# Delta-rule inverse of a hybrid trunk layer: 32x32 blocks on five levels instead of one

## Chip, cores and metric

The kernel runs on one core of a Trainium2 chip. The time is the device time of one execution in microseconds (us), the median of three runs. A second, profiled execution gives the trace; its span is the time from its first instruction to its last.

## What is computed

The reference is one step of a network of two shared-weight layers over 512 latent and 128 context tokens (640 rows, in five tiles of 128). Each layer has four mixers: A, a chunked gated delta rule in two directions; B, long convolutions; C and D, attention. The change lies in mixer A, which has four heads. Per head, direction and chunk of 64 tokens it solves a unit triangular system:

```
lower = jnp.where(strict, jnp.einsum('bhnid,bhnjd->bhnij', kb, k) * decay, 0.0)
sol = lax.linalg.triangular_solve(lower + jnp.eye(CHUNK, dtype=jnp.float32), rhs,
                                  left_side=True, lower=True, unit_diagonal=True)
```

## The kernel before, in words

Everything is laid out by hand: each engine has its own program, written in the order in which it runs, and semaphores join them. All products with the large weights are sums of three products of split operands (`h_hi*w_hi + h_lo*w_hi + h_hi*w_lo`); the trace calls them proj<-h_hi,w_hi and so on.

Instead of solving, mixer A inverts the triangular matrices by doubling, `A_levels(h)`. Level `lv` makes the inverses of diagonal blocks of 2^(lv+1) rows out of those of 2^lv rows. A tile of 128 tokens is worked in two halves of 64 rows (`HALVES`) in both directions (`d`), so one level has 2 directions, 5 tiles and 2 halves. A level has two blocks of small fp32 matmuls on TensorE (PE). `A_level_q` makes the product of the matrix `dec` with the present inverse `Y`: 20 matmuls of 64x64. ScalarE (ACT) copies it, negated, into `Q`. `A_level_d` makes the two products of `Q` with `X`, 40 matmuls of 64x64. VectorE (DVE) then takes the new entries into `X` and `Y` with `copy_predicated` under the masks of the level (`update`, lines 2311 and 2312). Level 0 has only half of the second block (20 matmuls by the identity `ident_64`). Levels 5 and 6, which join blocks of 32 and 64 rows, have code of their own.

Up to level 4 the inverse is block diagonal in blocks of at most 32 rows, so products of 32x32 diagonal blocks (`QUARTERS`, four per tile instead of two halves) hold all that is needed; the rest of the PSUM tile `mix` lies outside the masks. The kernel before does so on level 2 (`FOURS = 2`) of heads 0 to 2, not on the others. Head 3 takes 64x64 on all these levels.

Between the blocks stand pieces of the projection of the next head, the fills: `eighths` of six 128x320 matmuls each. After the first block of a level there is one, after the second one there are two (three after level 4), after level 0 two. They cover the answers of ACT and DVE. Every fp32 matmul of the small blocks is two weight loads (PEld LDWEIGHTS) and two MATMUL instructions in the trace, so 20 matmuls of 64x64 are 40 records of each kind; a matmul of a fill is one of each. The two layers run the same program text twice in a row, unrolled, and mixer A's head loop is unrolled too.

Of the kernel before, what the change touches and what calls it, by code (L numbers as in the profile page):

```python
# [20 lines left out]
TILES, KT, HEADS, W = 5, 8, 4, 128  # L21
# [23 lines left out]
def program(nc, I, O):  # L45
# [3 lines left out]
    with ctx:  # L49
        def sb(name, shape, dt=f32):  # L50
            return ctx.enter_context(nc.sbuf_tensor(name, [shape[0], int(np.prod(shape[1:]))], dt))

        def view(t, *dims, at=0):

            n = int(np.prod(dims))
            names = "abcd"[:len(dims)]
            return t[:, at:at + n].rearrange(
                "p (" + " ".join(names) + ") -> p " + " ".join(names),
                **{x: d for x, d in zip(names[:-1], dims[:-1])}) if len(dims) > 1 else t[:, at:at + n]
# [19 lines left out]
        ident_64 = sb("ident_64", [128, 64])  # L79
# [171 lines left out]
        X, Y = a.take(2, TILES, 64), a.take(2, TILES, 64)  # L251
# [10 lines left out]
        Q, Q_mid, Q_last = view(area, 2, TILES, 64, at=a_q), view(area, TILES, 32, at=a_q), view(area, TILES, 64, at=a_q + HALF)  # L262
        SIDES = (slice(0, 64), slice(64, 128))
        HALVES = tuple((c, slice(0, 64)) for c in SIDES)
        QUARTERS = tuple((slice(32 * i, 32 * i + 32), slice(32 * (i % 2), 32 * (i % 2) + 32)) for i in range(4))
        FOURS = 2
        A_GATES = {0: (0, 3), 14: (3, 4), 18: (4, 5), 22: (5, 6)}
        A_pairs = tuple((d, QUARTERS[2 * i + d][0], QUARTERS[2 * i + 1 - d][0], QUARTERS[d][1], QUARTERS[1 - d][1])
                        for d in range(2) for i in range(2))
# [446 lines left out]
        def _(pe):  # L716
# [4 lines left out]
            def mm(out, l, r, start=True, stop=True):  # L721
                return T.matmul(out, l, r, start=start, stop=stop)  # L722
# [34 lines left out]
            for layer in range(DEPTH):  # L757
# [198 lines left out]
                def A_level_q(h, lv):  # L956

                    e = h * A_STEPS + 2 * lv
                    for d in range(2):
                        pe.wait_ge(A_x.sem, A_x.at(layer, e + (d - 1)))  # L960
                        for t in range(TILES):
                            for c, w in QUARTERS if lv == FOURS and h < HEADS - 1 else HALVES:
                                at = 1024 * d + 64 * t + w.start
                                last = mm(M[c, at:at + w.stop - w.start], dec[c, d, t, c], Y[c, d, t, w])
                        last.then_inc(A_q.sem, A_q.step)

                def A_level_d(h, lv):
                    e = h * A_STEPS + 2 * lv
                    for d in range(2):
                        pe.wait_ge(A_qn.sem, A_qn.at(layer, e + (d + 1)))  # L970
                        if lv == 0:
                            pe.wait_ge(A_q0.sem, A_q0.at(layer, h + 1))
                        blocks = QUARTERS if lv == FOURS and h < HEADS - 1 else HALVES
                        for t in range(TILES if lv else 0):
                            for c, w in blocks:
                                at = 1024 * d + 64 * t + w.start
                                mm(M[c, at:at + w.stop - w.start], Q[c, d, t, w], X[c, d, t, w])
                        for t in range(TILES):
                            for c, w in blocks:
                                at = 1024 * d + 512 + 64 * t + w.start  # L980
                                l, r = (X[c, d, t, w], Q[c, d, t, w]) if lv else (Q[c, d, t, w], ident_64[c, :])
                                last = mm(M[c, at:at + w.stop - w.start], l, r)
                        last.then_inc(A_d.sem, A_d.step)

# [39 lines left out]
                def A_levels(h):  # L1024
# [11 lines left out]
                    fill(0, 2)  # L1036
                    pe.wait_ge(A_su.sem, A_su.at(layer, 5 * h))
                    A_level_d(h, 0)
                    fill(2, 4)
                    for lv, (first, mid, end) in enumerate(((4, 5, 7), (7, 8, 10), (10, 11, 13), (13, 14, 17), (17, 18, 20), (20, 22, 24)), 1):  # L1040
                        if lv < LEVELS - 2:
                            A_level_q(h, lv)
                        elif lv == LEVELS - 2:
                            A_mid_q(h)
                        else:
                            A_last_q(h)
                        fill(first, mid)
                        if lv < LEVELS - 2:
                            A_level_d(h, lv)
                        elif lv == LEVELS - 2:  # L1050
                            A_mid_d(h)
                        else:
                            A_last_d(h)
                        if lv == 1 and h:
                            pe.wait_ge(proj_taken.sem, proj_taken.at(layer, min(4 * h + 5, 15)))
                            if h == HEADS - 1:
                                pe.wait_ge(proj_taken.sem, proj_taken.at(layer, 16))
                            A_out(h - 1, psum_a[int(h == HEADS - 1)])
                        fill(mid, end)
# [1923 lines left out]
```

## Time and profile before

| what | value |
|---|---|
| median of 3 runs | 2581.85 us |
| lowest, highest | 2580.23, 2582.1 us |
| span of the profiled execution | 2586.7 us (no other time of it is on record) |
| PE busy, share of the span | 2487.4 us, 96% |
| weight loads (PEld) busy | 2355.7 us, 91% |
| DVE, ACT, POOL busy | 1332.7, 977.9, 341.7 us |
| small matmuls of 64x64, records (without level 0) | 3440, 118.8 us |
| small matmuls of 32x32, records | 2240, 27.2 us |
| fetches on queue q8, kind "instruction" | 172, 2.82 MB |

PE, the matmuls, and PEld, the weight loads, are one instruction stream and overlap. "Idle before" is the time in which the engine did nothing ahead of an instruction; behind the arrow stands what ended it. "issue" there means that nothing in the profile, neither a semaphore nor data, was waited for. Matmuls are pipelined, so the time that a block takes is read from its start to the start of what follows it, not from its length.

### The profile page before, as it was taken

The numbers are of one execution on the slowest core, as the hardware profiler recorded it, in microseconds if no ns is written. First come the engines' busy times: TensorE is split into PE (matmuls) and PEld (weight loads), VectorE is DVE, ScalarE is ACT, GpSimd is POOL, SyncE is SP. The second block draws the span as 40 slices with busy tenths as digits, with TensorE's granted clock in tenths as the row PEclk, the third lists the DMA queues.
The fourth block names the chain that finished last, engine by engine and source line by source line (L and its number), as shares of the span: only waits on it lengthen the run. The fifth ranks groups of instructions, "written<-read, shape, count | busy, mean of one in ns | idle before, by whom it ended". The sixth has DMA issues, their size and how long they took to land. (4 is left out here: it accounts for less than half of the span.)

```text
span 2586.7 us, 56706 instructions
## 1 busy us (share of the span) xinstructions
PE 2487.4 (96%) x23368; PEld 2355.7 (91%) x23368; DVE 1332.7 (52%) x2335; ACT 977.9 (38%) x1830; POOL 341.7 (13%) x406
## 2 busy tenths in 40 slices
PE   6999989999999999999989999999999999999998
PEld 4889889999999999879988888899999999988898
DVE  4565653577434434653555566527773344356544
ACT  3545432333234424442354454233332353254422
POOL 1332211000011101110013332100000010011000
PEclk9999999999999999999999999999999999999999
DMA  7111104111234333213221100231113332222132
GB/s 262 38 39 33 36 20 145 58 35 48 103 106 98 85 107 96 64 54 141 86 82 37 39 31 31 66 120 37 50 50 92 86 89 84 84 65 71 42 108 82
DMA packets 55687, 193.89 MB, mean 75 GB/s; under 512 B 9032, under 2 KB 9198, under 8 KB 55328
## 3 DMA queue, kind: packets, MB, share of 16 engines
q1 hardware_dynamic: 40304, 147.34, 16.9%
q0 software_dynamic: 15152, 43.24, 6.3%
q8 instruction: 172, 2.82, 0.4%
q14 instruction: 59, 0.48, 0.1%
HBM read 177.97 MB, written 8.39 MB: 72 GB/s over the span
## 5 line engine op out<-in xcount | busy, mean ns | idle before, releaser
L722 PE MATMUL proj<-h_hi,w_hi 128*128 128x320 f32 x3072 | 749.6, 324 | 8.7 <-DVE h_lo L2104 5.2
L722 PE MATMUL proj<-h_lo,w_hi 128*128 128x320 f32 x3072 | 703.9, 310 | 0.0
L722 PE MATMUL proj<-h_hi,w_lo 128*128 128x320 f32 x3072 | 699.5, 310 | 0.0
L2104 DVE TENSOR_TENSOR w_lo<-raw,w_hi 128x1024 fp32r<-128x1024 f32 x232 | 289.8, 1249 | 527.6 <-ACT w_hi L1562 527.4
L722 PEld LDWEIGHTS proj<-h_hi,w_hi 128*128 128x128 f32 x3072 | 503.6, 189 | 32.0 <-issue 11.4
L722 PEld LDWEIGHTS proj<-h_lo,w_hi 128*128 128x128 f32 x3072 | 516.3, 189 | 0.0
L722 PEld LDWEIGHTS proj<-h_hi,w_lo 128*128 128x128 f32 x3072 | 514.5, 188 | 0.0
L722 PE MATMUL mix<-area 64*64 64x64 f32 (+7 forms) x8176 | 474.2, 238 | 29.4 <-DVE area L2312 12.1
L722 PEld LDWEIGHTS mix<-area 64*64 64x64 f32 (+4 forms) x8176 | 402.3, 142 | 89.1 <-issue 46.3
L1562 ACT ACTIVATE w_hi<-raw 128x1024 fp32r<-128x1024 f32 x232 | 245.6, 1059 | 587.1 <-PE proj L722 397.3
L1562 ACT ACTIVATE area<-mix 128x384 f32<-128x384 f32 (+8 forms) x422 | 186.8, 466 | 570.1 <-PE mix L722 415.3
L2104 DVE TENSOR_TENSOR area<-area 128x512 f32<-128x512 f32 (+6 forms) x234 | 159.4, 712 | 29.1 <-ACT merged L2031 14.3
L476 POOL TENSOR_TENSOR stat<-stat,neg_half 128x5 f32<-128x5 f32 (+2 forms) x40 | 50.6, 1265 | 698.0 <-DVE stat L2273 271.2
L725 PE MATMUL mix<-ident,area 128*128 128x128 f32 x748 | 113.5, 278 | 17.5 <-issue 7.1
L722 PE MATMUL mix<-y_hi,w_hi 128*128 128x320 f32 x512 | 120.8, 317 | 2.4 <-DVE merged L2104 1.7
L1562 ACT ACTIVATE area<-proj 128x128 f32<-128x128 f32 (+8 forms) x248 | 80.7, 392 | 104.0 <-PE proj L722 95.4
L722 PE MATMUL mix<-y_lo,w_hi 128*128 128x320 f32 x512 | 116.6, 309 | 0.0
L722 PE MATMUL mix<-y_hi,w_lo 128*128 128x320 f32 x512 | 116.6, 309 | 0.0
L725 PEld LDWEIGHTS mix<-ident,area 128*128 128x128 f32 x748 | 88.2, 142 | 29.8 <-issue 14.9
L1968 ACT ACTIVATE area<-mix,stat 128x640 f32<-128x640 f32 (+1 forms) x80 | 56.0, 705 | 103.9 <-DVE stat L2694 103.8
L722 PEld LDWEIGHTS mix<-y_hi,w_hi 128*128 128x128 f32 x512 | 84.0, 188 | 7.7 <-issue 5.2
L2104 DVE TENSOR_TENSOR area<-area,mix 128x384 f32<-128x384 f32 (+3 forms) x112 | 46.6, 455 | 76.8 <-ACT area L1562 76.8
(292 smaller groups left out, 2755.4 us busy)
## 6 DMA issues: line engine op xcount, KB each, us to landing
raw<-in_w_in SPq DMA_DIRECT2D x128, 512.0 KB, 3.5
raw<-in_w_mb SPq DMA_DIRECT2D x96, 512.0 KB, 3.5
raw<-in_w_mod POOLq DMA_DIRECT2D x32, 512.0 KB, 4.7
area<-in_bias POOLq DMA_DIRECT2D x64, 128.0 KB, 4.7
raw<-in_w_out SPq DMA_DIRECT2D x16, 512.0 KB, 3.5
merged<-in_w_mod SPq DMA_DIRECT2D x10, 512.0 KB, 7.2
out_x<-area SPq DMA_DIRECT2D x10, 512.0 KB, 2.6
area<-in_x_sample SPq DMA_DIRECT2D x2, 2048.0 KB, 8.8
```

What stands on the lines that cost most here:

```text
L476: P.tensor_tensor(stat[:, at:at + cols], stat[:, at:at + cols], neg_half[:, 0:cols], ALU.pow).then_inc(done_sig.sem, done_sig.step)
L722: return T.matmul(out, l, r, start=start, stop=stop)
L725: return T.transpose(out, src, ident[:, :])
L1562: return A.activation(out, x, ACT.Copy, scale=scale)
L1968: last = A.activation(D_p[:, i % 2, j, cols], D_scores[j][:, cols], ACT.Exp, bias=stat[:, 2 * m + j:2 * m + j + 1], accum_out=stat[:, 16 + ...
L2104: return V.tensor_tensor(out, a_, b_, op)
```

## The change

The first five levels (0 to 4) of heads 0 to 2 take 32x32 blocks, in both layers. On level 0 the identity is cut to the columns of the block. Levels 5 and 6, head 3, the copies on ACT and DVE, the masks, the fills, the semaphores and the order of the blocks stay as they are.

```
-        FOURS = 2
@@ A_level_q
-                            for c, w in QUARTERS if lv == FOURS and h < HEADS - 1 else HALVES:
+                            for c, w in QUARTERS if h < HEADS - 1 else HALVES:
@@ A_level_d
-                        blocks = QUARTERS if lv == FOURS and h < HEADS - 1 else HALVES
+                        blocks = QUARTERS if h < HEADS - 1 else HALVES
@@ A_level_d, level 0
-                                l, r = (X[c, d, t, w], Q[c, d, t, w]) if lv else (Q[c, d, t, w], ident_64[c, :])
+                                l, r = (X[c, d, t, w], Q[c, d, t, w]) if lv else (Q[c, d, t, w], ident_64[c, w])
```

On TensorE, from level 0 of head 0 (the first row) to the first block of level 1 (the last), the order of before is:

```order
L722 MATMUL mix<-ident,area 64x64 x20
L722 MATMUL proj<-h_hi,w_hi 128x320 x2
L722 MATMUL proj<-h_lo,w_hi 128x320 x2
L722 MATMUL proj<-h_hi,w_lo 128x320 x2
L722 MATMUL proj<-h_hi,w_hi 128x320 x2
L722 MATMUL proj<-h_lo,w_hi 128x320 x2
L722 MATMUL proj<-h_hi,w_lo 128x320 x2
L722 MATMUL mix<-area 64x64 x20
```

and of the changed kernel, whose lines are numbered one lower:

```order
L721 MATMUL mix<-ident,area 32x32 x40
L721 MATMUL proj<-h_hi,w_hi 128x320 x2
L721 MATMUL proj<-h_lo,w_hi 128x320 x2
L721 MATMUL proj<-h_hi,w_lo 128x320 x2
L721 MATMUL proj<-h_hi,w_hi 128x320 x2
L721 MATMUL proj<-h_lo,w_hi 128x320 x2
L721 MATMUL proj<-h_hi,w_lo 128x320 x2
L721 MATMUL mix<-area 32x32 x40
```

Nothing moves past anything else; each block has twice as many matmuls of a quarter of the size. The same place on TensorE two levels later, from the second block of level 2 to that of level 3 of head 0, before:

```order
L722 MATMUL mix<-area 32x32 x80
L722 MATMUL proj<-h_hi,w_hi 128x320 x2
L722 MATMUL proj<-h_lo,w_hi 128x320 x2
L722 MATMUL proj<-h_hi,w_lo 128x320 x2
L722 MATMUL proj<-h_hi,w_hi 128x320 x2
L722 MATMUL proj<-h_lo,w_hi 128x320 x2
L722 MATMUL proj<-h_hi,w_lo 128x320 x2
L722 MATMUL mix<-area 64x64 x20
L722 MATMUL proj<-h_hi,w_hi 128x320 x2
L722 MATMUL proj<-h_lo,w_hi 128x320 x2
L722 MATMUL proj<-h_hi,w_lo 128x320 x2
L722 MATMUL mix<-area 64x64 x40
```

and changed:

```order
L721 MATMUL mix<-area 32x32 x80
L721 MATMUL proj<-h_hi,w_hi 128x320 x2
L721 MATMUL proj<-h_lo,w_hi 128x320 x2
L721 MATMUL proj<-h_hi,w_lo 128x320 x2
L721 MATMUL proj<-h_hi,w_hi 128x320 x2
L721 MATMUL proj<-h_lo,w_hi 128x320 x2
L721 MATMUL proj<-h_hi,w_lo 128x320 x2
L721 MATMUL mix<-area 32x32 x40
L721 MATMUL proj<-h_hi,w_hi 128x320 x2
L721 MATMUL proj<-h_lo,w_hi 128x320 x2
L721 MATMUL proj<-h_hi,w_lo 128x320 x2
L721 MATMUL mix<-area 32x32 x80
```

Level 2 stays; level 3 becomes like it.

## Rows read from the trace of the kernel before

**Rows 1.** The page's first part: busy time, share of the span, instructions.
```profile
PE 2487.4 (96%) x23368; PEld 2355.7 (91%) x23368; DVE 1332.7 (52%) x2335; ACT 977.9 (38%) x1830; POOL 341.7 (13%) x406
```
**Rows 2.** Groups by shape on PE: busy us, mean ns | idle us before, releasers.
```profile
L722 PE MATMUL mix<-area 64*64 64x64 f32 x3440 | 118.8, 224 | 15.2 <-DVE area L2312 12.1 <-ACT area L1562 2.3 <-DVE area L2304 0.7
...
L722 PE MATMUL mix<-area 32*32 32x32 f32 x2240 | 27.2, 193 | 7.5 <-issue 6.5 <-ACT area L1562 0.8
```
**Rows 3.** Timeline of PE, head 0, layer 0, levels 2 and 3: start, length.
```profile
116.30 0.91 PE L722 MATMUL mix<-area 32*32 32x32 f32 x80
117.14 0.56 PE L722 MATMUL proj<-h_hi,w_hi 128*128 128x320 f32 x2
...
118.21 1.25 PE L722 MATMUL mix<-area 32*32 32x32 f32 x121
120.90 0.54 PE L722 MATMUL mix<-area 32*32 32x32 f32 x39 [1.44 <-issue]
121.37 0.56 PE L722 MATMUL proj<-h_hi,w_hi 128*128 128x320 f32 x2
...
123.32 1.38 PE L722 MATMUL mix<-area 64*64 64x64 f32 x40
124.63 0.56 PE L722 MATMUL proj<-h_hi,w_hi 128*128 128x320 f32 x2
...
125.71 2.55 PE L722 MATMUL mix<-area 64*64 64x64 f32 x80
128.19 0.56 PE L722 MATMUL proj<-h_hi,w_hi 128*128 128x320 f32 x2
...
130.14 1.38 PE L722 MATMUL mix<-area 64*64 64x64 f32 x40
...
135.01 0.56 PE L722 MATMUL proj<-h_hi,w_hi 128*128 128x320 f32 x2
...
137.84 0.55 PE L722 MATMUL mix<-area 32*32 32x32 f32 x40
```
**Rows 4.** Timeline of PE, head 1, layer 0: level 1's first block, level 2's second.
```profile
182.37 1.38 PE L722 MATMUL mix<-area 64*64 64x64 f32 x40
...
193.88 0.57 PE L722 MATMUL mix<-area 32*32 32x32 f32 x43 [1.06 <-issue]
```
**Rows 5.** Windows: PE busy (count), PEld busy (count), others, clock, DMA share.
```profile
120.89:193.88 72.99, 70.96 (x1144) 65.85 (x1145) 43.75 (x82) 33.93 (x76) 19.40 (x13) 1.00 0.11 35
```
**Rows 6.** DMA view of the same window, the instruction queue.
```profile
q8 instruction: 9, 0.15, 0.7%
```
**Rows 7.** DMA view, 116 to 124 us in 40 slices; nothing but two fetches.
```profile
GB/s 0 0 0 0 0 0 0 0 0 0 82 0 0 0 0 0 0 0 0 0 0 0 0 0 0 0 0 0 0 0 82 0 0 0 0 0 0 0 0 0
...
q8 instruction: 2, 0.03, 1.8%
```
**Rows 8.** DMA view, 1392 to 1400 us (head 0, layer 1), likewise.
```profile
GB/s 348 451 184 62 0 0 0 0 0 0 0 0 82 0 0 0 0 0 0 0 0 0 0 0 0 0 0 0 0 82 0 0 0 0 0 0 0 0 0 0
```
**Rows 9.** Timeline of PE, head 0, layer 0: level 0 and level 1's first block.
```profile
102.76 1.38 PE L722 MATMUL mix<-ident,area 64*64 64x64 f32 x40 [0.38 <-ACT area L1562]
104.07 0.56 PE L722 MATMUL proj<-h_hi,w_hi 128*128 128x320 f32 x2
...
108.56 0.80 PE L722 MATMUL mix<-area 64*64 64x64 f32 x20 [1.73 <-DVE area L2312]
```
**Rows 10.** Timeline of DVE: level 0's last copy, head 0 and head 1.
```profile
108.00 0.51 DVE L2312 COPY_PREDICATED area<-level,mix 128x320 f32<-128x320 uint8 x1
...
182.05 0.50 DVE L2312 COPY_PREDICATED area<-level,mix 128x320 f32<-128x320 uint8 x1
```
**Rows 11.** Windows, columns as in rows 5: head 0 after its wait, both layers, head 3.
```profile
109.20:112.00 2.80, 2.80 (x28) 2.40 (x25) 2.14 (x1) 1.89 (x6) 2.63 (x3) 0.52 0.00 0
...
1381.10:1416.30 35.20, 32.68 (x836) 29.94 (x836) 20.55 (x28) 13.51 (x40) 10.41 (x5) 1.00 0.10 33
...
320.00:345.00 25.00, 20.35 (x536) 19.05 (x534) 16.56 (x29) 10.06 (x29) 9.44 (x6) 0.93 0.05 14
```

## The prediction

> **What bounds the kernel.** I began with the busy shares: PE works in 96% of the span, and no other engine in more than 52% [rows 1]. So a microsecond that PE saves or loses counts in full, unless PE then waits for something else. Next I took PE's groups by shape, because they hold both kinds of block side by side: 3440 records of 64x64 and 2240 of 32x32 [rows 2]. The reader is to look at the idle time: 6.5 us before the 32x32 blocks have the releaser "issue", that is, no semaphore and no data. The timeline says where: in the second block of level 2, PE stops for 1.44 us in head 0 after 121 records, and for 1.06 us in head 1 [rows 3, 4]. Then I asked what stands at a fixed place there. From the one stop to the other PE runs 1144 matmuls and 1144 or 1145 weight loads [rows 5], and in the same window the instruction queue makes 9 fetches of together 0.15 MB [rows 6]. 2288 records and some 16 semaphore instructions, which are not counted as busy, are 9 times 256. I read this as: PE's program comes in pieces of 256 instructions, the next piece is asked for when PE enters the present one, and PE stops at the border if the next isn't there yet.
>
> **The price of a piece.** Around such a stop two fetches stand 4.0 us apart in head 0 of layer 0 (slices of 0.2 us, at 118.0 and 122.0) and 3.4 us in layer 1 (1394.4 and 1397.8) [rows 7, 8]. While PE is held back by the supply, this distance is the period of the supply. I take the middle, 3.7 us per 256 instructions, and keep both ends. The fills ask for far less (24 instructions in 1.95 us, 121.37 to 123.32) [rows 3], and so does a level in 64x64: 2*(40+6+80+12) = 276 instructions in 6.82 us, where the supply would take 4.0.
>
> **Work that goes.** First blocks: 1.31 us for 20 matmuls of 64x64 (123.32 to 124.63), 0.84 us for 40 of 32x32 (116.30 to 117.14), so 0.47 less. Second blocks: 2.48 us (125.71 to 128.19) against 3.16 - 1.44 = 1.72 us without the stop (118.21 to 121.37), so 0.76 less [rows 3]. Levels 1, 3 and 4 save 1.23 each. Level 0 isn't in the trace with 32x32; its shape is that of a first block, also 1.31 us for 40 records (102.76 to 104.07) [rows 9], and I give it the same 0.47; bounds are 0 and 0.66 (half the block). One head saves 3 * 1.23 + 0.47 = 4.16 us, six (three heads, two layers) 25.0 us.
>
> The 32x32 records start 0.84 / 80 = 10.5 ns apart, because neighbours lie in different parts of the array [rows 3]. The Trainium skill ("TensorE: Matmul & The Clock Gate", Wait — 56ns, not 53.3ns?) says against this change that matmuls never start closer than about 25 ns, however few columns they have. By that a first block would take 2.0 us instead of 0.84, and the change would lose some 44 us. The rows at level 2 decide against it here, so I give it no more than 1 in 100.
>
> **Waits of PE for DVE that take some of it.** In the first block of level 1 the second direction waits for DVE's last copy of level 0. In head 0 that copy ends at 108.51, and PE has already waited 1.73 us for it [rows 9, 10]. DVE doesn't come sooner, so what level 0 and the first half of the next block save there (0.47 + 0.23) becomes wait: 2 * 0.70 = 1.4 us. In head 1 the copy ends at 182.55 and the second half begins at 182.37 + 0.66 = 183.03 [rows 4, 10]. It would now begin at 182.37 - 0.47 + 0.42 = 182.32, 0.23 too soon; with the signal's way I take 0.25, four times 1.0 us. At the other levels DVE and ACT have fills of 1.07 and 1.95 us to answer in, and these stay. Left: 25.0 - 2.4 = 22.6 us.
>
> **Instructions that come.** Each 64x64 matmul becomes two of 32x32, each of four instructions. Level 3 grows from 276 to 2*(80+6+160+12) = 516 instructions, like level 2. Its work falls to 6.82 - 1.23 = 5.59 us, but the supply needs 516/256 * 3.7 = 7.46 us. So PE will stop 1.88 us per level on levels 1, 2 and 3. Level 4 has a third fill: 528 instructions, 7.63 us of supply for 7.70 - 1.23 = 6.47 us of work, 1.16 us of stops. That is 6.8 us per head. From it goes what is in store when the dense part begins: at least nothing, on average half a piece, worth 1.85 us, since a border may fall anywhere; I take 0.8, near the middle of the two. Level 0 neither fills nor drains it (160 + 24 instructions in 0.84 + 1.95 us, where the supply takes 2.7). 6.0 * 6 = 36 us of stops, where there were 6.5: 29.5 more. The new fetches are another 4800 / 256 = 19 of 16 KB; beside 72 GB/s of weight traffic that is nothing, but they have to pass that traffic.
>
> **Sum.** 29.5 - 22.6 = +6.9 us. The profiled span is 2586.7 us, and only that is on record of that execution; it is 4.9 us over the median, by the run and by what the profile adds. I carry the difference over: 2581.85 + 7 = 2589 us. With the period at 3.4 us the stops are 1.27 per level and 0.54, less 0.8: 3.55 * 6 = 21.3, and the sum is 14.8 - 22.6 = -8 us. With 4.0 us it is 2.47 and 1.78, less 0.8: 8.4 * 6 = 50, so +21 us. The price is steep: 0.1 us of period is 0.8 us per head, 5 us in all.
>
> **Rivals.**
> - *Each level stops once, as level 2 does.* 1.09 us (6.5 / 6) on four levels in six heads is 26 us, 19.6 more; 19.6 - 22.6 = -3 us, 2579. For it: that is what the trace shows of a 32x32 level. Against it: there the level before was in 64x64 and left a full stock, and now two such levels follow each other. It lies within 0.2%.
> - *The supply doesn't bind.* Then 22.6 us go, 2559. The Trainium skill ("Runtime: NRT & Kernel Launch", Instruction fetch mechanics) says that PE holds 2048 instructions, is refilled in blocks of 256, and that the fetch is hidden behind the issue rate. The block size agrees with the 9 fetches [rows 5, 6]; a store of 2048 would leave no stop at level 2, and there are six. Something of it may still hold, if the stops have a cause at level 2 only.
> - *The clock falls.* This ends slower. After the wait of head 0 in layer 0 the granted clock was 0.52, that is the lower level for nearly all of 2.8 us, which took some 1.4 us; in layer 1, with the same wait, it stayed at 1.00; head 3, which stays in 64x64 and waits more, had 0.93 [rows 11]. If stops of 1 to 2 us twice in each level bring one such fall per head, that adds 6 * 1.4 = 8 us to the forecast: 2597. Against it: level 2 with its stops has not done so. It decides from the point at which the stops come closer than today's one per head.
> - *The stops stay but are longer*, since weight loads of 512 KB are under way: that is the end of 4.0 us, 2603.
>
> **How the numbers follow.** Runs of this kernel differ by 1.9 us, so I count as no change what lies within 0.2%, 5.2 us (2576.7 to 2587.0). Forecast by the supply 0.50, its own range 2578 to 2600, of which seven tenths lie above 2587 (0.35) and 0.11 in the band, 0.04 below. Once per level 0.23: 0.17 in the band, 0.06 below. Supply not binding 0.07, below. Clock 0.12 and longer stops 0.08, both above. Slower 0.55, same 0.28, faster 0.17. Range: down to 2575, up to 2605; outside are the case of the free supply and the far end of the long stops.
>
> **What would show it.** In the profile after, 32x32 records rise from 2240 by 4800 to 7040. Their idle time before with releaser "issue" should be some 30 to 40 us instead of 6.5, in stops of 0.5 to 2 us at borders 256 instructions apart, about two per level. A first block without a stop should take 0.84 us on every level, and a second one 1.72. In head 0 the wait for line 2311 of the changed kernel, DVE's copy, should grow from 1.73 to about 2.4 us. Level 3 of head 0 should last 7.0 to 7.5 us instead of 6.82. If levels 1 to 4 last about 5.6 us, the supply is not what I think. If the stops are there but no longer than a fetch's rest of 1 us each and one per level, the first rival is right. A granted clock below 1.00 in heads 1 and 2 would speak for the third.

## The result, and the profile after

| | before | changed |
|---|---|---|
| median (runs) | 2581.58 us (4) | 2604.34 us (4) |
| lowest, highest | 2580.23, 2582.1 | 2601.2, 2607.63 |
| profiled execution: span | 2586.7 | 2599.6 |

The change makes the kernel slower: ratio 1.0084, 95% interval 1.0069 to 1.0098, or +22.8 us of the medians. 2589 was forecast; the sign is right, the size is three times as large, and the range to 2605 just holds it. The four executions of before differ by 1.9 us, but 31 more that ran beside the first experiments lie between 2576.2 and 2590.5 us, so 1.9 us was too narrow a measure of the noise. The two traces differ by only 12.9 us, since before's profiled execution lay above its runs and the changed one's (2601.2 us) at the bottom of its own.

The page's first part, of the changed kernel; it answers to [rows 1]:

```profile
PE 2467.4 (95%) x25768; PEld 2332.0 (90%) x25768; DVE 1333.0 (51%) x2335; ACT 977.4 (38%) x1830; POOL 341.8 (13%) x406
```

PE has 20 us less to do, and the span is longer. Its groups by shape, after; they answer to [rows 2]:

```profile
L721 PE MATMUL mix<-area 32*32 32x32 f32 x6560 | 81.4, 196 | 42.4 <-issue 36.1 <-DVE area L2311 4.7 <-ACT area L1561 0.8
L721 PE MATMUL mix<-area 64*64 64x64 f32 x1280 | 45.5, 225 | 11.6 <-DVE area L2311 8.6 <-ACT area L1561 2.3 <-DVE area L2303 0.7
...
L721 PE MATMUL mix<-ident,area 32*32 32x32 f32 x480 | 5.7, 193 | 2.3 <-ACT area L1561 2.3
```

6560 + 480 = 7040 records of 32x32, and 36.1 us of stops by "issue" where there were 6.5. PE's timeline of head 0, layer 0, from level 0 to the second block of level 4, after (start, length; rows of the fills left out but for some); it answers to [rows 3, 9]:

```profile
102.47 0.95 PE L721 MATMUL mix<-ident,area 32*32 32x32 f32 x80 [0.38 <-ACT area L1561]
103.36 0.56 PE L721 MATMUL proj<-h_hi,w_hi 128*128 128x320 f32 x2
...
108.27 0.55 PE L721 MATMUL mix<-area 32*32 32x32 f32 x40 [2.12 <-DVE area L2311]
...
109.82 0.97 PE L721 MATMUL mix<-area 32*32 32x32 f32 x91
111.79 0.79 PE L721 MATMUL mix<-area 32*32 32x32 f32 x69 [0.99 <-issue]
...
114.46 0.60 PE L721 MATMUL mix<-area 32*32 32x32 f32 x47
116.35 0.47 PE L721 MATMUL mix<-area 32*32 32x32 f32 x33 [1.28 <-issue]
...
117.81 0.95 PE L721 MATMUL mix<-area 32*32 32x32 f32 x89
120.08 0.81 PE L721 MATMUL mix<-area 32*32 32x32 f32 x71 [1.32 <-issue]
...
122.77 0.59 PE L721 MATMUL mix<-area 32*32 32x32 f32 x44
123.66 0.50 PE L721 MATMUL mix<-area 32*32 32x32 f32 x36 [0.30 <-issue]
...
125.17 0.94 PE L721 MATMUL mix<-area 32*32 32x32 f32 x86
127.40 0.83 PE L721 MATMUL mix<-area 32*32 32x32 f32 x74 [1.29 <-issue]
...
130.11 0.57 PE L721 MATMUL mix<-area 32*32 32x32 f32 x42
131.13 0.53 PE L721 MATMUL mix<-area 32*32 32x32 f32 x38 [0.45 <-issue]
...
132.67 0.92 PE L721 MATMUL mix<-area 32*32 32x32 f32 x84
135.97 0.84 PE L721 MATMUL mix<-area 32*32 32x32 f32 x76 [2.38 <-issue]
```

From level 2 on each level of 516 instructions is cut twice here, and the cut wanders by two or three records, four to six instructions, per level, where 516 - 512 asks for four. Over the six heads there are 34 stops on 24 levels, fewer than the two per level that were forecast: in layer 0's head 2 and layer 1's head 0 about every second border passes without one.

The stops can be placed exactly by counting all of PE's records from the start of the trace: matmuls, weight loads, and the semaphore, register and branch instructions of its sequencer. Head 0's seven stops come at records 1985, 2241, 2497, 2752, 3008, 3264 and 3520, which is 255 or 256 apart. The same holds in all eight traces whose levels have stops (this one, before, after_again, every_other, second_blocks, shifted, double_fill_32 and first_and_level2): their 134 stops in the levels of heads 0 to 2 all stand at the same place of a count by 256, at 192 or 193 in layer 0 and at 62 or 63 in layer 1.

The borders at 116.35, 120.08, 123.66, 127.40 and 131.13 stand 3.58 to 3.74 us apart. The one before them, from 111.79, takes 4.56, the one behind them 4.84. In both a load of 512 KB of weights stands between the border and the fetch; elsewhere in this head's dense part the fetch goes out 1.1 to 1.3 us after the border. The DMA view of 132 to 138 us in slices of 0.15 us shows the last one: the tail of a load of 512 KB of weights fills the engines first, and the fetch (one slice of 109) goes out behind it, at 133.7, 2.5 us after PE entered the piece.

```profile
GB/s 164 382 437 382 328 410 410 437 55 0 27 109 0 0 0 0 0 0 0 0 0 0 0 0 0 0 0 0 0 0 0 0 0 109 0 0 0 0 0 0
```

Windows of the changed kernel (columns as in rows 5): heads 0 and 1 of layer 0 and head 0 of layer 1 from level 0 to level 4, and the end of head 1; they answer to [rows 11].

```profile
102.47:139.58 37.11, 26.74 (x1130) 23.66 (x1131) 20.00 (x28) 12.51 (x36) 10.37 (x5) 1.00 0.10 32
180.83:216.81 35.98, 29.61 (x1135) 26.72 (x1136) 22.33 (x35) 12.20 (x36) 11.71 (x6) 0.91 0.11 36
209.50:216.40 6.90, 5.84 (x112) 5.78 (x112) 4.04 (x7) 0.00 (x0) 0.00 (x0) 0.51 0.02 5
1386.40:1424.30 37.90, 29.90 (x1130) 26.86 (x1130) 20.00 (x28) 12.35 (x36) 10.37 (x5) 0.86 0.09 32
```

Head 0 took 35.08 us for the same (102.76 to 137.84) [rows 3, 9]. In head 1 the clock falls to its lower level (half speed, 0.51 in the window from 209.50) during a stop of 2.64 us, one microsecond before PE goes on:

```profile
210.56 1.50 PE L721 MATMUL mix<-area 32*32 32x32 f32 x96 [2.64 <-issue]
```

### The profile page after: what moved, and what is told of

Its sections match the earlier page's. It is cut to its first block and busy times, and to the rows that moved or that the text cites. A ratio compares the mean times of both kernels' runs of the same rounds, so it can differ in the third digit from the quotient of the medians.

```text
span 2599.6 us, 61506 instructions
## 1 busy us (share of the span) xinstructions
PE 2467.4 (95%) x25768; PEld 2332.0 (90%) x25768; DVE 1333.0 (51%) x2335; ACT 977.4 (38%) x1830; POOL 341.8 (13%) x406
## 3 DMA queue, kind: packets, MB, share of 16 engines
q1 hardware_dynamic: 40304, 147.34, 16.6%
## 5 line engine op out<-in xcount | busy, mean ns | idle before, releaser
L721 PE MATMUL mix<-area 32*32 32x32 f32 (+7 forms) x10336 | 455.2, 224 | 60.8 <-issue 36.1
L721 PEld LDWEIGHTS mix<-area 32*32 32x32 f32 (+4 forms) x10336 | 380.2, 129 | 124.7 <-issue 79.1
```

## The experiments

Ratios are to the kernel before, run on the same chip beside each.

**halves_all.** `QUARTERS if False` in both functions: 64x64 throughout levels 0 to 4.

> No 32x32 blocks on levels 0 to 4 at all: level 2 of heads 0 to 2 goes back to 64x64. Supply (256 instructions in about 3.7 us, PE stops at a border that comes sooner): a level then has 276 instructions in 6.8 us, so no stop with releaser issue is left in levels 1 to 4; the six stops of together 6.5 us go, and 6 * 1.23 = 7.4 us of work come: +1 us against the kernel before, within 0.2%. Rival, 32x32 blocks are simply cheaper and the stops are noise of one run: +7 us. Clock: the granted clock in heads 1 and 2 stays 1.00, since the stops are gone.

1.0003 (0.9993 to 1.0014), 2583.27 us. In its trace no "issue" is left before the small blocks (2.9 us before other `mix` matmuls, outside the levels, stay in every kernel), and the clock stays up in the levels of all six heads. Heads 0 and 1 of layer 0:

```profile
103.50:136.90 33.40, 31.67 (x614) 29.21 (x615) 19.92 (x28) 12.50 (x36) 10.35 (x5) 1.00 0.10 34
178.10:210.10 32.00, 31.98 (x619) 29.68 (x622) 21.86 (x35) 12.53 (x36) 11.71 (x6) 1.00 0.11 39
```

So level 2 in 32x32, which the kernel before has, gave nothing that the runs show: what its work saves its stops take.

**first_blocks, first_again.** They are one kernel, run twice. Beside the identity cut to the block on level 0, its difference from before is

```
-    for c, w in QUARTERS if lv == FOURS and h < HEADS - 1 else HALVES:      # A_level_q
+    for c, w in QUARTERS if h < HEADS - 1 else HALVES:
-    blocks = QUARTERS if lv == FOURS and h < HEADS - 1 else HALVES          # A_level_d
+    blocks = QUARTERS if lv == 0 and h < HEADS - 1 else HALVES
```

> 32x32 on level 0 and in the first block (dec times Y) of levels 1 to 4 of heads 0 to 2; second blocks all in 64x64. Supply: 160 + 12 + 160 + 24 = 356 instructions per level in 6.35 us of work, the supply takes 5.1, and a full piece is never run in under 3 us, so stops vanish or stay under 0.3 us each. Against the kernel before: work 6 * (4 * 0.47 - 0.47 + 0.47) less, counted as 6 * 1.88 = 11.3 us less for levels 0, 1, 3, 4, then 6 * 0.76 = 4.6 us more for level 2's second block, 6.5 us of stops less, 2.4 us of waits for DVE more: -11 us. Rival, every level with 32x32 blocks stops some 1.1 us whatever their number: 4 * 6 * 1.09 - 6.5 = 19.6 more and about -4 of work and waits: +15 us.

0.9965 (0.9949 to 0.9981), 2574.56 us.

> The kernel with 32x32 in first blocks and level 0 alone (first_blocks) once more, for a narrower interval: 0.9965 of the kernel before was measured (-9 us), the supply's account said -11. Expected 0.995 to 0.998, no stop with releaser issue in levels 0 to 4, and no half clock window there but the one after head 0's wait for DVE.

0.9965 (0.9953 to 0.9977), 2574.26 us against 2583.14. PE's group in first_again, with no "issue" in it:

```profile
L722 PE MATMUL mix<-area 32*32 32x32 f32 x2720 | 34.4, 194 | 5.9 <-DVE area L2312 4.4 <-ACT area L1562 0.8
```

The half of the change that needs few instructions per microsecond gains 9 us, some 2 us short of the account. The rival "each level with 32x32 stops" is out.

**every_other.** `lv % 2 == 0 and h < HEADS - 1` in both functions.

> Both blocks in 32x32 on levels 0, 2 and 4, both in 64x64 on levels 1 and 3. Supply: a 64x64 level leaves a full store, so the dense levels stop once each, 0.3 to 1.1 us, and stops sum to 7 to 13 us where the changed kernel has about 36. Work 6 * (1.23 + 0.47) = 10.2 us less than before, waits for DVE 2.4 more, stops 0.5 to 6.5 more: -1 to -7 us against before, and some 25 us faster than the changed kernel. Rival, the loss comes from the clock that falls after any stop: no fewer falls than in the changed kernel, time near 2600.

1.0012 (1.0000 to 1.0023), 2584.86 us. All "issue" before PE's `mix` blocks is 14.4 us, 39.0 in the changed kernel. Both numbers hold the 2.9 us outside the levels, so 11.5 us are the levels' (7 to 13 expected). It is some 20 us faster than the changed kernel, as the supply wants; against before it is 3 us slower, 4 us outside the range that was expected. The clock falls twice in its levels, beside the fall after head 0's wait.

```profile
PE mix L722 <- issue: 14.4, 12, 2.8
```

**second_blocks.** 32x32 only in `A_level_d` of levels 1 to 4 (`lv and h < HEADS - 1`).

> 32x32 only in the second blocks of levels 1 to 4 of heads 0 to 2; level 0 and all first blocks in 64x64. Supply: 80 + 12 + 320 + 24 = 436 instructions per level in 6.06 us of work where the supply takes 6.3: stops of 12 to 20 us in sum, most of 0.5 to 1.5 us, all inside second blocks. Work: 18 * 0.76 = 13.7 less, 6 * 0.47 = 2.8 more: -10.9; stops 6 to 13 more: -5 to +2 us against before. Rival, the first blocks are the costly ones (a switch of the array between shapes): then this kernel would be the fast one at -11.

1.0019 (1.0008 to 1.0030), 2587.96 us; 18.3 us of "issue". Without the 2.9 us outside the levels that is 15.4 us, in the range; three more stops, 3.4 us together, stand in fills and not in second blocks as expected. The time is above its range by 4 us. In its levels the clock is at the lower level in five stretches beside the one after head 0's wait, so both kernels with stops lost more than the stops. The rival, that the first blocks are costly, is refuted by first_blocks.

**after_again.** The changed kernel.

> The changed kernel once more, beside the others, for its stops and its clock. Supply: the stops with releaser issue in the small blocks sum to 30 to 40 us again, at the same places, since the borders lie fixed in the program. Clock: windows of half clock that begin inside levels 0 to 4 of heads 0 to 2, some five or more per run, at other places than last time. Time 2600 to 2607 us. If the supply alone made the loss, heads 0 to 2 of both layers would be some 7 us longer than in the kernel before; with the clock some 15.

1.0080 (1.0063 to 1.0098), 2602.89 us, and 41.7 us of stops in the 32x32 blocks. The stretch from level 0 to level 4, summed over heads 0 to 2 of both layers, is 217.1 us, and 213.2 in the first trace of the changed kernel; before has 196.6, halves_all 194.5, first_again 183.0. That is 16.6 to 20.5 us over before, not 7. At the lower clock these stretches spend 17.1 us here, 23.9 in the first trace, 6.8 in before and none in halves_all and first_again.

**shifted.** The kernel before with this ahead of PE's first matmul:

```
+            for _ in range(128):
+                held(pe)          # pe.sem_inc(passed_PE, 1)
```

> The kernel before with 128 semaphore increments at the very start of TensorE's program, in the time in which it waits for its first weights; nothing else differs. Supply: each border of 256 instructions comes 128 instructions earlier in the program's work. In layer 0, heads 0 to 2, no full piece lies in level 2's blocks any more and the stop of 1.0 to 1.4 us after some 120 records of the second block goes, at most 0.2 us stay; in layer 1 a piece then lies wholly inside the second block, and one stop of about 2.4 us stands some 4 instructions before its end instead of 0.7 to 1.4 us in its middle. Sum 6 to 9 us, time within 0.2% of before. Rival, the stops belong to level 2 or to its 32x32 blocks: they stay where they are, 1.0 to 1.4 us each in both layers.

1.0069 (1.0054 to 1.0085), 2601.94 us. The stops are where the supply put them. Layer 0, level 2 of head 0: the second block runs through, and a small stop has wandered into level 3, into a 64x64 block. Layer 1: all 160 records but one, then 2.45 us.

```profile
130.39 1.58 PE L724 MATMUL mix<-area 32*32 32x32 f32 x160
133.85 0.62 PE L724 MATMUL mix<-area 64*64 64x64 f32 x13
134.63 1.03 PE L724 MATMUL mix<-area 64*64 64x64 f32 x27 [0.17 <-issue]
...
1404.39 1.62 PE L724 MATMUL mix<-area 32*32 32x32 f32 x159
1408.46 0.21 PE L724 MATMUL mix<-area 32*32 32x32 f32 x1 [2.45 <-issue]
```

The stops of the levels sum to 7.0 us, 6 to 9 expected. "Time within 0.2%" failed for a dull reason: I had taken the 128 increments to be hidden. They take longer than the wait for the first weights, so PE's first matmul starts at 31.68 us, some 15 us late; the kernel is 20 us slower. Summed over the six heads the levels take 198.3 us, 196.6 before. And in these levels the clock falls at the long stops alone: three stretches at half clock begin in layer 1 within 0.4 us of the ends of its three stops of 2.45, 1.95 and 2.18 us, none in the levels of layer 0's heads 0 to 2, where no stop is over 0.2 us.

```profile
1408.40:1412.00 3.60, 3.54 (x13) 3.18 (x13) 3.03 (x5) 0.00 (x0) 0.00 (x0) 0.54 0.02 5
1394.00:1404.00 10.00, 8.28 (x220) 7.58 (x217) 6.87 (x7) 3.26 (x10) 7.04 (x4) 1.00 0.15 54
```

**double_fill_32, double_fill_64.** The changed kernel and halves_all, with `eighths` in `fill` issuing a second piece of the same projection beside each (shortened):

```
-    last = product(u, h_hi_v, h_lo_v, KT, 0, psum_a[u % 2], part=(i,))
+    for k in ((i, 1) if i == 0 else (min(i, KT - 2), i)):      # in the fills of heads 0 to 2
+        last = product(u, h_hi_v, h_lo_v, KT, 0, psum_a[u % 2], part=(k,))
```

> The changed kernel with each fill between the blocks of levels 0 to 6 of heads 0 to 2 made twice as long by repeating its matmuls, so the projections of heads 1 to 3 of mixer A hold wrong sums. More instructions than the changed kernel (a level has 552 instead of 516) but 8.2 us of work instead of 5.6. Supply: stops fall from about 36 to about 16 us in sum, since a piece that holds fill lasts longer. The kernel comes out some 16 us FASTER than the same with 64x64 blocks (double_fill_64), where without doubling it was 21 us slower. Rival, 32x32 blocks stop PE by themselves: as many and as long stops as in the changed kernel, and 15 to 20 us slower than double_fill_64.

> The kernel with 64x64 on all levels (halves_all) with the same doubled fills; the projections of heads 1 to 3 of mixer A hold wrong sums. No stops in levels 0 to 4. 24 fills of 0.88 us in six heads: some 120 us above 2583, about 2700. The stretches of head 0 that wait for DVE lose their wait.

2684.79 us (1.0394, 1.0379 to 1.0409) and 2701.98 us (1.0462, 1.0446 to 1.0477): with twice the fill the 32x32 version is 17.2 us the faster, where without it it is 21 us the slower. Same blocks, same shapes, more instructions, more time for each piece; "issue" before `mix` blocks falls from 39.0 to 15.5 us. This is the sharpest answer to "32x32 blocks stop PE by themselves".

```profile
PE mix L721 <- issue: 15.5, 21, 2.3
```

**first_all_heads.** `QUARTERS` in all first blocks and level 0, head 3 too.

> The same in all four heads. Head 3 has no fills, so PE waits for ACT and DVE at each block and 320 instructions per level run in some 5 us, where the supply takes 4.6: no stop, or under 0.3 us. Its chain goes through one direction's part of each block, 0.65 us that becomes 0.42: 0.2 to 0.5 us per level and layer, so 2 to 5 us faster than first_again. Rival, PE waits there anyway and the chain of DVE sets the pace: no difference.

0.9963 (0.9950 to 0.9976), 2573.91 us: no difference from first_again. The rival was right. DVE's copy paces head 3: the waits of PE for it grow from 13.3 us in first_again to 15.9 us.

**first_and_level2.** first_again with `lv in (0, 2)` in `A_level_d`.

> first_again with level 2's second block in 32x32 as well, as the kernel before has it. Work 4.6 us less than first_again. Supply: one level of 516 instructions, six stops of 0.3 to 1.7 us again, 6 to 10 us in sum: 2 to 6 us slower than first_again, more if the clock falls after them. Rival without the supply: 4.6 us faster than first_again.

0.9965 (0.9952 to 0.9978), 2573.93 us, where 2 to 6 us over first_again were expected. The levels do take 3.6 us longer in its trace (186.6 against 183.0 us, with 7.4 us of stops of 0.3 to 1.7 us). The granted clocks on record show what gave it back: the mean of its five executions is 0.9954, that of first_again's six 0.9937, which is worth some 4 us of 2574. Why its clock stayed up more isn't shown. One of its stops stands in a fill, between two 128x320 matmuls, so a stop doesn't need a 32x32 block on either side:

```profile
118.67 0.46 PE L722 MATMUL proj<-h_hi,w_hi 128*128 128x320 f32 x2
120.10 0.45 PE L722 MATMUL proj<-h_lo,w_hi 128*128 128x320 f32 x2 [0.97 <-issue]
```

## Why the prediction was right or wrong

- *Pieces of 256, the next asked for on entering the present one.* Held. All stops stand at the same place of a count by 256, shifted moved them by 128 instructions, double_fill_32 filled the gaps. That the fetch is asked for on entering is read from its start, 1.1 to 1.3 us behind the border in head 0 where no load is in the way. Of the Trainium skill's two statements ("Runtime: NRT & Kernel Launch", Instruction fetch mechanics) the blocks of 256 agree with the 255 or 256 records between stops; that the fetch is hidden does not, with 36.1 us of stops, and I took it for a rival rightly.
- *The period of 3.7 us.* Held in the clear. In both traces of the changed kernel 28 pieces lie between two stops with no weight load between border and fetch, and take 3.46 to 4.07 us. What I left as a rival, fetches behind weight loads, comes on top: 13 pieces, all but one of 4.0 to 5.4 us.
- *Stops of 36 us.* 36.1 and 41.7 us in the two traces. *Work saved.* A first block that PE runs through takes 0.84 us, as forecast (head 1, 191.13 to 191.97); level 0 takes 0.89 (102.47 to 103.36) and gave 0.42 rather than 0.47. *Wait for DVE in head 0.* 2.12 us, 2.4 expected. *Level 3 of head 0.* 7.34 us (122.77 to 130.11), 7.46 expected. With 36.1 us of stops these terms sum to +7 us again, with 41.7 to +13.
- *The clock.* This is the step that failed, in that the sum has no term for it. I gave the falling clock 12 in 100 and a case of its own, with "level 2 with its stops has not done so" against it. That sentence was false, and the trace of before would have told me: in head 1 of layer 1 the clock falls 1.1 us behind level 2's stop of 1.43 us. The stop in before, and windows behind it and with it:

```profile
1470.17 0.79 PE L722 MATMUL mix<-area 32*32 32x32 f32 x69 [1.43 <-issue]
...
1471.20:1474.60 3.40, 3.40 (x20) 3.07 (x20) 3.04 (x5) 0.00 (x0) 0.42 (x1) 0.51 0.02 5
1467.80:1471.20 3.40, 1.97 (x163) 1.81 (x163) 2.35 (x4) 0.90 (x4) 3.24 (x3) 1.00 0.00 0
```

It is a second term and not another case. In the first trace the levels are 16.6 us longer, 7 of it by the terms above, so 9 to 10 us are left. They spend 23.9 us at the lower of the two levels, half speed, and before's 6.8: 17 us more at half speed are 8.5 us. In after_again 20.5 us are 13 by the terms and 5 by the clock (17.1 us), and 2 to 3 are open.

All executions together say the same, since each has its mean granted clock on record. An execution's time multiplied by one minus that clock is what it lost to the lower level: 27 us on average in the four of the changed kernel and 23 in the six of after_again, against 14 to 16 in three sets of before. So the clock is 8 to 13 us of the 21 to 23 between the kernels, and 9 to 12 are left for stops less work, where I had 7.

shifted shows that it is the long stops that bring the falls: it is before with stops of 1.95 to 2.45 us in layer 1 in place of 0.74 to 1.43, and there are three falls at them where before has one. In the levels of heads 0 to 2 of all eight traces with stops, a fall begins between 1 us before and 1.7 us after the end of 21 of the 35 stops of more than 1.4 us, and at none of the 99 shorter ones. It is no strict rule, then; the stop of 2.38 us in head 0 above is followed by none. All other falls there come after head 0's wait for DVE, and so do the only ones in the five traces without stops (halves_all, first_blocks, first_again, first_all_heads, double_fill_64). What decides between one long stop and the next isn't shown.

- *Luck.* The range held by 0.7 us. Its upper end was made for another case, fetches that take 4.0 us throughout (2603), and not for stops of the forecast's length with a falling clock beside them.
- *The carried difference.* I took the 4.9 us between before's span and its median as a constant. In the runs after, one execution's time is 1.6 us over its span (2601.2 to 2599.6), so before's trace came from an execution some 6.7 us slower than its median (2588.3 by that rule), and the changed one from one 3.1 us faster than its own. 12.9 + 6.7 + 3.1 = 22.7 us: that is the gap of the medians. The forecast doesn't suffer by it, as it puts a difference on the median, but two traces alone would show little more than half of the loss. The clock is what was slow in that execution of before: its mean was 0.992, some 21 us lost, where the other sets of before lose 14 to 16.

## What to carry to other kernels

Count instructions per microsecond before splitting matmuls into smaller ones. If a stretch asks for more than one piece of 256 per period of the fetch (here 3.7 us, 70 per microsecond), the split buys stops instead of time, and the stops, here those of more than 1.4 us, can pull down the clock. Split where few instructions stand close together and leave the long burst alone: in the first blocks only, that is 2574 us, 0.9965 of before and 30 us under the change.

## What the runs showed of the hardware that I hadn't expected

A semaphore increment on PE's queue isn't free: in shifted's trace the 128 take effect 0.15 us apart, from 12.09 to 31.49 us, and moved the first matmul from some 17 to 31.68 us. A fetch of instructions that meets a weight load comes later: in the changed kernel's two traces the period was 4.0 to 5.4 us in 12 of 13 such pieces and 3.46 to 4.07 in the 28 others. And one stop of 1.4 to 2.9 us in the middle of dense work was enough in 21 of 35 cases for the clock to fall to its lower level at it. By the length of the stretch at half speed a fall cost 1.7 us in 19 of them and 3.4 us in two.
